# A local-attention layer with sinks: half of the queries projected first, keys and values second

## The chip, the cores and the metric

The kernel runs on one core of one Trainium2 chip. The metric is the device time of one execution of the whole program, in microseconds (us). It is a forward pass through four layers; the change touches the third of them only.

## What is computed

A sequence of 512 tokens with 1,024 features goes through four layers. Each layer is a token mixer and a convolutional feed-forward network (FFN), both between RMS norms and added to the residual h. The mixers are, in order, a sparse attention ("nsa"), a stick-breaking attention ("sb"), a local attention with sinks ("swa") and "nsa" again. The third one, cut to what matters:

```
def swa_sink_mixer(h, w_in, sinks, w_out):        # H=16 query heads, G=2 key/value heads, dh=64, W=128
    q, k, v = jnp.split(h @ w_in, [H * dh, H * dh + G * dh], axis=-1)      # 1024 | 128 | 128 columns
    ...                                           # query t sees the W keys up to t
    s = einsum(q, k window) * scale - slopes * dist
    m = jnp.maximum(max(s), sink)
    e = jnp.where(mask, jnp.exp(s - m), 0.0)
    p = e / (jnp.sum(e) + jnp.exp(sink - m))
    return (p @ v window) @ w_out
```

The layer's input is rms_norm(h) times a gain.

## The kernel before, in words

**Data.** Activations lie with features on the partitions: h, and the scaled input as eight chunks of 128 features by 512 tokens. Every f32 operand of a large product is split into a high and a low part of the reduced format (xh and xl for activations, w_hi and w_lo for weights), and a product is three matmuls: high by high, high by low, low by high. The norm's factor 1/rms of each token isn't needed for the products: it is applied afterwards, as rb (per column) or rt (per token on partitions), when a result leaves PSUM.

**Weight units.** Weights come in units of 128 x 1024 f32 through a ring of four slots (RING). SP's queue loads w_raw of a unit once the unit four before it has been split. ScalarE (ACT) makes w_hi (L252, `split_hi`), once the unit four before it has been used (units_done); VectorE (DVE) makes w_lo (L258, `split_lo`). `split_his(u, n)` and `split_los(u, n)` do this for units u+3 to u+n+2 (AHEAD is 3). On each engine everything is in program order, so a split that waits holds back what stands behind it.

**Panels.** A panel is a group of four PSUM banks, and panels alternate between the lower and the upper half of PSUM. Panel p starts when panel p-2 has been read out (`panel_free`; the table MIX_READS says which engines read each panel). The layer's query projection is two panels of four units each, 96 matmuls of 512 columns with 128 x 128 weights: 4 units x 2 chunks x 4 banks x 3. Keys and values are two units: for each of the eight chunks three matmuls of 512 columns (keys, weights stationary) and twelve of 128 columns (values, activations stationary; 4 token groups x 3).

**The start of a layer.** When the FFN before has ended, ACT forms rn (L433, L434), and then for each of the eight chunks DVE forms dh (L454) and h (L460), ACT xh (L472) and the square (L477), DVE xl (L440); GpSimd (POOL) adds up the squares (L484, L488). TensorE (PE) can follow chunk by chunk in two ways. `first_panel` uses a chunk's xh for eight matmuls (L319, L320) as soon as ACT has made it, and its xl (L323) when that is there. The other way, which the swa layer has, waits for xl of a pair of chunks (x_ready). After the last square, `pe_rsum` sums over partitions (L370) and over tokens (L373), and `act_rb` makes rt and rb (L381 to L386).

**The swa layer before.** PE: keys and values (panel p0, units u0 and u0+1), `pe_rsum`, first half of the queries (`after_rsum`, panel p0+1, L348 to L350), second half (`x_panel`, panel p0+2, L298 to L300), attention, output projection. DVE takes keys out into ktmp (L892), ACT spreads them into kh (L860), DVE makes kl (L870, L877); ACT takes out the values (L1611); DVE takes out the queries (L883). Attention waits for both query halves, k_ready and v_ready. The sb and nsa layers start with `first_panel` on queries (or keys), and so does every FFN.

Of the kernel before, what the change touches and what calls it, by code (L numbers as in the profile page):

```python
# [12 lines left out]
P = 128  # L13
# [6 lines left out]
DH = 64  # L20
# [20 lines left out]
MIX_PANELS = {"nsa": 8, "sb": 6, "swa": 3}  # L41

MIX_READS = {"nsa": [(1, 0), (1, 0), (0, 1), (1, 0), (1, 1), (0, 0), (1, 1), (0, 0)], "sb": [(1, 0)] * 4 + [(0, 1)] * 2,
             "swa": [(1, 1)] + [(1, 0)] * 2}

L1_UNITS = (8, 9, 11, 12, 14, 15, 17, 18)
QB_UNITS = (10, 13, 16, 19)
# [55 lines left out]
def hybrid_layers(nc, ins, out, kinds=KIND):  # L103
# [7 lines left out]
    with ExitStack() as ctx:  # L111
# [103 lines left out]
        def panel_free(pe, p, i=None, step=0):  # L215


            if p >= 2:
                pe.wait_ge(evac_v, at(i, step, v_after[p - 1]))
                if s_after[p - 1]:  # L220
                    pe.wait_ge(evac_s, s_after[p - 1])

        def bank(p, o):
            return psum[:, 4 * (p % 2) + o, :]
# [36 lines left out]
        def split_his(act, u, count):  # L261

            count = min(count, plan.units - AHEAD - u)
            turns = count // 4 if count >= 8 else 0
            if turns:
                with act.Fori(0, turns) as i:
                    for k in range(4):
                        split_hi(act, u + k + AHEAD, i)
            for k in range(4 * turns, count):
                split_hi(act, u + k + AHEAD)  # L270
# [95 lines left out]
        def pe_rsum(pe, n, p, by_token):  # L366

            pe.wait_ge(ssh_done, 8 * (n + 1))
            panel_free(pe, p)
            mm = nc.tensor.matmul(bank(p, 3), ones[:], ss[:], start=True, stop=True)  # L370
            if by_token:
                for t in range(TC):
                    mm = nc.tensor.matmul(bank(p, 2)[:, t:t + 1], ss[:, t * P:(t + 1) * P], ones[:, 0:1],  # L373
                                          start=(t == 0), stop=(t == TC - 1), skip_group_check=True)
            mm.then_inc(rsum_done, 1)
# [446 lines left out]
        def three(out, lh, ll, rh, rl, start, stop, **kw):  # L822

            nc.tensor.matmul(out, lh, rh, start=start, stop=False, **kw)  # L824
            nc.tensor.matmul(out, ll, rh, start=False, stop=False, **kw)  # L825
            return nc.tensor.matmul(out, lh, rl, start=False, stop=stop, **kw)  # L826
# [748 lines left out]

        def pe_swa(pe, l):
            n, u0, p0 = 2 * l, plan.mix_u[l], plan.mix_p[l]
            panel_free(pe, p0)
            for j in range(2):
                u = u0 + j  # L1580
                pe.wait_ge(split_done, u + 1)
                for q in range(4):
                    c = 4 * j + q
                    if q % 2 == 0:
                        pe.wait_ge(x_ready, 8 * n + c + 2)
                    wk, wv = slice(256 * q, 256 * q + P), slice(256 * q + P, 256 * q + 2 * P)
                    three(bank(p0, 0), w_hi[:, u % RING, wk], w_lo[:, u % RING, wk], xh[:, c, :], xl[:, c, :], c == 0, c == DC - 1)
                    for t in range(TC):
                        tok = slice(t * P, (t + 1) * P)
                        mm = three(bank(p0, 2)[:, tok], xh[:, c, tok], xl[:, c, tok], w_hi[:, u % RING, wv],  # L1590
                                   w_lo[:, u % RING, wv], c == 0 and t == 0, c == DC - 1, skip_group_check=True)
                mm.then_inc(units_done, 1)
            pe_rsum(pe, n, p0 + 1, True)
            after_rsum(pe, p0 + 1, u0 + 2, n, True)
            x_panel(pe, p0 + 2, u0 + 6, n)
            panel_free(pe, p0 + 4)
            pe.wait_ge(k_ready, kc_before[l] + 1)
            pe.wait_ge(v_ready, kvs_before[l] + 1)
            pe_attention(pe, l, "swa")
            pe_out(pe, l, ot)  # L1600

        def act_swa(act, ch, l):
            n, u0, p0 = 2 * l, plan.mix_u[l], plan.mix_p[l]
            split_his(act, u0 + 1, 1)
            act_rb(act, ch, n, p0 + 1, True)
            split_hi(act, u0 + 2 + AHEAD)
            act_k(act, l, 0, 0, 1, 2)
            for t in range(TC):
                for g in range(SG):
                    src = bank(p0, 2)[:, t * P + g * DH:t * P + (g + 1) * DH]  # L1610
                    m = ch.then(nc.scalar.activation(vt[0][:, t, g * P:(g + 1) * P].rearrange("p (e d) -> p e d", d=DH),  # L1611
                                                     src.unsqueeze(1).to_broadcast([P, 2, DH]), ACT.Copy, scale=rt[:, t:t + 1]))
            act.wait_ge(s_chain, m)
            act.sem_inc(evac_s, 1)
            act.sem_inc(v_ready, 1)
            split_his(act, u0 + 3, 7)
            act.wait_ge(k_ready, kc_before[l] + 1)
            act.wait_ge(q_done, qn_before[l] + 2)
            act.wait_ge(mix_landed, 16 * small_before[l])
            act_attention(act, l, "swa")  # L1620
            act_turn_o(act, l, plan.out_p[l])
            act_out(act, l)

        def dve_swa(dve, ch, l):
            n, u0, p0 = 2 * l, plan.mix_u[l], plan.mix_p[l]
            split_los(dve, u0 + 1, 1)
            dve.wait_ge(rb_done, n + 1)
            split_lo(dve, u0 + 2 + AHEAD)
            dve_k(dve, ch, l, 0, p0, u0 + 2, 1)
            dve.wait_ge(kt_done, kc_before[l] + 1)  # L1630
            dve.sem_inc(evac_v, 1)
            dve_k_low(dve, ch, l, 0, 0, 1, 2)
            split_los(dve, u0 + 3, 3)
            dve_q(dve, ch, l, 0, p0 + 1, u0 + 6, -SCALE, qt)
            split_los(dve, u0 + 6, 4)
            dve_q(dve, ch, l, 1, p0 + 2, u0 + 10, -SCALE, qt)
            dve.wait_ge(mix_landed, 16 * small_before[l])
            dve.wait_ge(v_chain, ch.then(nc.vector.tensor_scalar(neg_sinks[:], sinks[:], -1.0, None, ALU.mult)))
            dve_attention(dve, ch, l, "swa")
            dve_turn_o(dve, l, plan.out_p[l])  # L1640
            dve_out(dve, l)
# [315 lines left out]
def layout(x, norm_g, nsa_w_in, nsa_cmp_pos, nsa_cmp_w1, nsa_cmp_w2, nsa_w_out, sb_w_in, sb_w_out,  # L1957
           swa_w_in, swa_sinks, swa_w_out, ffn_w_up, ffn_conv_w, ffn_conv_b, ffn_w_down):

    a = {}  # L1960
    a["x"] = x[0].T.reshape(DC, P, T).transpose(1, 0, 2)
    a["norm_g"] = norm_g.reshape(DEPTH * 4, DC, P).transpose(2, 0, 1)
    a["conv_w"] = ffn_conv_w.reshape(DEPTH * 3, 2 * FC, P).transpose(2, 0, 1)
    a["conv_b"] = ffn_conv_b.reshape(DEPTH, 2 * FC, P).transpose(2, 0, 1)

    up = ffn_w_up.reshape(DEPTH, DC // 2, 2, P, 2, UP_PANELS, 256)
    a["w_up"] = up.transpose(0, 5, 1, 3, 2, 4, 6).reshape(-1, P, 1024)

    w1 = nsa_cmp_w1.reshape(-1, 2, 4, 4, P, CMP_HID).transpose(0, 1, 2, 4, 3, 5).reshape(-1, 8, P, 1024)
    a["nsa_in"] = np.zeros((len(w1) * 28, P, 1024), np.float32)  # L1970
    for j, w in enumerate(nsa_w_in):
        u = units(w[:, :2560])
        a["nsa_in"][28 * j:28 * j + 4] = u[8:12]
        a["nsa_in"][28 * j + 4:28 * j + 8] = u[:4]
        a["nsa_in"][[28 * j + x for x in L1_UNITS]] = w1[j]
        a["nsa_in"][[28 * j + x for x in QB_UNITS]] = u[4:8]
        a["nsa_in"][28 * j + 20:28 * j + 28] = u[12:]
    a["nsa_gw"] = nsa_w_in[:, :, 2560:].reshape(-1, DC, P, 48).transpose(0, 2, 1, 3)
    w2 = nsa_cmp_w2.reshape(-1, 2, 2, P, DH).transpose(1, 0, 3, 2, 4)
    a["nsa_w2k"] = np.concatenate([w2[0], w2[0]], axis=-1)  # L1980
    a["nsa_w2v"] = w2[1]
    a["nsa_pos"] = nsa_cmp_pos.reshape(-1, 2, CMP_LEN // 2, P).transpose(0, 3, 1, 2)
    a["nsa_out"] = np.concatenate([units(w) for w in nsa_w_out])
    a["sb_in"] = np.concatenate([units(w) for w in sb_w_in])
    a["sb_out"] = np.concatenate([units(w) for w in sb_w_out])
    swa_kv = swa_w_in[:, :, 1024:].reshape(-1, 2, 4, P, 256).transpose(0, 1, 3, 2, 4).reshape(-1, 2, P, 1024)
    a["swa_in"] = np.concatenate([x for kv, w in zip(swa_kv, swa_w_in) for x in (kv, units(w[:, :1024]))])
    a["swa_out"] = np.concatenate([units(w) for w in swa_w_out])
    a["sinks"] = np.broadcast_to(swa_sinks[0], (P, H))
    a["w_down"] = np.concatenate([units(w) for w in ffn_w_down])  # L1990
    return a
# [40 lines left out]
```

## Time and profile before

| | us |
|---|---|
| three runs, median (lowest, highest) | 2855.12 (2848.9, 2857.5) |
| the profiled execution, whole | 2857.26 |
| its span | 2855.5 |
| PE busy in the span | 2727.1 (96%) |
| DVE, ACT, POOL busy | 1685.5, 1205.6, 362.1 |
| PE's granted clock, mean | 0.971 of full |

The span runs from the first to the last instruction that the profile shows; 1.8 us of the execution lie around it. Start times below are us from the span's start. The swa layer's mixer begins at about 1501 and its output projection ends at about 1713. Full speed of PE's clock is 2.4 GHz, and a granted clock of 0.50 is 1.2 GHz.

### The profile page before, as it was taken

How to read it: one execution, taken by the hardware profiler on the slowest of the kernel's cores; microseconds unless marked ns; L12 is line 12 of the kernel's file. 1: busy time of each engine (PE TensorE's matmuls, PEld its weight loads, DVE VectorE, ACT ScalarE, POOL GpSimd, SP SyncE). 2: the span in 40 equal slices, each digit the busy share in tenths (PEclk: the TensorE clock that was granted, in tenths of full speed). 3: DMA queues.
4: the chain of work that ended last, by engine and by line, in shares of the span. 5: the costliest groups of instructions: out<-in, count | busy, mean ns of one | idle time of the engine just before them, and what ended most of it. 6: DMA issues, size and time to landing. Idle time of an engine off the chain costs nothing.

```text
span 2855.5 us, 38959 instructions
## 1 busy us (share of the span) xinstructions
PE 2727.1 (96%) x13616; PEld 2258.7 (79%) x13616; DVE 1685.5 (59%) x2837; ACT 1205.6 (42%) x2051; POOL 362.1 (13%) x314
## 2 busy tenths in 40 slices
PE   8989999999999999999999899999999899999997
PEld 6878878888786667888887777888878788788886
DVE  7568767764442224776525758665275787576743
ACT  4356544443223443444323644443243565444431
POOL 1012111110000000211001102111010122111100
PEclk9989999999998999999996999999999999999999
DMA  4300023333232002233322012333324000233331
GB/s 155 124 23 2 1 78 107 98 95 101 77 100 70 1 1 67 92 100 95 96 75 71 31 60 83 100 97 96 90 78 133 30 1 1 67 118 95 95 96 52
DMA packets 62200, 210.83 MB, mean 74 GB/s; under 512 B 8688, under 2 KB 10736, under 8 KB 62064
## 3 DMA queue, kind: packets, MB, share of 16 engines
q1 hardware_dynamic: 62064, 209.01, 23.7%
q8 instruction: 86, 1.41, 0.2%
q14 instruction: 50, 0.41, 0.0%
HBM read 206.88 MB, written 2.10 MB: 73 GB/s over the span
## 4 chain that ended last, share of the span: by engine, by line
PE 86%; DVE 9%; ACT 3%; issue 2%; DMA 0%; DVEq 0%; POOL 0%; SPq 0%; ACTq 0%; POOLq 0%
PE psum L298 19%; PE psum L299 19%; PE psum L300 19%; PE psum L969 5%; PE psum L959 2%; PE psum L824 2%; PE psum L1692 2%; PE psum L826 2%; PE psum L825 2%; DVE h L460 2%; PE psum L1703 2%; PE psum L1722 1%; PE psum L949 1%; DVE qs L1000 1%; PE psum L948 1%
## 5 line engine op out<-in xcount | busy, mean ns | idle before, releaser
L298 PE MATMUL psum<-xh,w_hi 128*128 128x512 f32 x1760 | 691.6, 393 | 3.0 <-DVE xl L1213 3.0
L299 PE MATMUL psum<-xh,w_lo 128*128 128x512 f32 x1760 | 686.8, 390 | 0.0
L300 PE MATMUL psum<-xl,w_hi 128*128 128x512 f32 x1760 | 686.5, 390 | 0.0
L258 DVE TENSOR_TENSOR w_lo<-w_raw,w_hi 128x1024 fp32r<-128x1024 f32 x226 | 280.5, 1253 | 532.9 <-ACT w_hi L252 530.5
L252 ACT ACTIVATE w_hi<-w_raw 128x1024 fp32r<-128x1024 f32 x226 | 235.7, 1057 | 584.8 <-PE psum L300 475.0
L298 PEld LDWEIGHTS psum<-xh,w_hi 128*128 128x128 f32 x1760 | 331.5, 188 | 74.4 <-issue 5.8
L299 PEld LDWEIGHTS psum<-xh,w_lo 128*128 128x128 f32 x1760 | 331.7, 188 | 69.9 <-issue 1.9
L300 PEld LDWEIGHTS psum<-xl,w_hi 128*128 128x128 f32 x1760 | 331.6, 188 | 69.1
L615 DVE TENSOR_TENSOR w_lo<-w_raw,w_hi 128x1024 fp32r<-128x1024 f32 x160 | 209.2, 1308 | 253.8 <-ACT w_hi L611 253.8
L298 PE MATMUL psum<-ah,w_hi 128*128 (+1 forms) x704 | 277.1, 394 | 0.0
L300 PE MATMUL psum<-al,w_hi 128*128 (+1 forms) x704 | 274.0, 389 | 0.0
L299 PE MATMUL psum<-ah,w_lo 128*128 (+1 forms) x704 | 273.9, 389 | 0.0
L611 ACT ACTIVATE w_hi<-w_raw 128x1024 fp32r<-128x1024 f32 x160 | 168.5, 1053 | 234.3 <-PE psum L300 234.3
L969 PE MATMUL psum<-v,pt 128*128 128x64 f32 x1504 | 212.4, 272 | 25.5 <-DVE pt L1072 25.3
L969 PEld LDWEIGHTS psum<-v,pt 128*128 128x128 f32 x1504 | 202.2, 194 | 42.1 <-DVE pt L1072 37.1
L585 POOL TENSOR_TENSOR cv<-cv 128x512 f32<-128x512 f32 x88 | 133.7, 1519 | 786.8 <-ACT cv L539 763.5
L1123 ACT ACTIVATE scores<-scores,mins 128x256 f32<-128x256 f32 (+1 forms) x320 | 171.4, 538 | 29.9 <-DVE mins L1017 22.6
L567 DVE SCALAR_TENSOR_TENSOR cv<-xo,conv_w,cv 128x512 f32<-128x512 f32 x176 | 169.5, 1003 | 0.6 <-DVE xo L558 0.6
L534 ACT ACTIVATE cv<-xo,conv_b,conv_w 128x512 f32<-128x512 f32 x176 | 129.2, 806 | 96.1 <-DVE xo L558 96.1
L1017 DVE CUSTOM_DVE_ANT_0 scores<-psum,tb 128x256 f32<-128x256 f32 (+1 forms) x320 | 148.8, 468 | 24.2 <-PE psum L949 22.1
L298 PEld LDWEIGHTS psum<-ah,w_hi 128*128 128x128 f32 x704 | 132.1, 188 | 29.1 <-issue 1.9
L299 PEld LDWEIGHTS psum<-ah,w_lo 128*128 128x128 f32 x704 | 132.2, 188 | 28.9 <-issue 1.9
(193 smaller groups left out, 4132.1 us busy)
## 6 DMA issues: line engine op xcount, KB each, us to landing
w_raw<-w_up SPq DMA_DIRECT2D x176, 512.0 KB, 3.6
w_raw<-w_down SPq DMA_DIRECT2D x88, 512.0 KB, 3.6
w_raw<-nsa_in SPq DMA_DIRECT2D x56, 512.0 KB, 4.0
w_raw<-sb_in SPq DMA_DIRECT2D x24, 512.0 KB, 3.7
w_raw<-nsa_out SPq DMA_DIRECT2D x16, 512.0 KB, 3.6
w_raw<-swa_in SPq DMA_DIRECT2D x10, 512.0 KB, 3.8
w_raw<-sb_out SPq DMA_DIRECT2D x8, 512.0 KB, 3.6
w_raw<-swa_out SPq DMA_DIRECT2D x8, 512.0 KB, 3.6
```

The source lines that it names most:

```text
L252: nc.scalar.activation(w_hi[:, u % RING, :], w_raw[:, u % RING, :], ACT.Copy).then_inc(hi_done, 1)
L258: nc.vector.tensor_tensor(w_lo[:, u % RING, :], w_raw[:, u % RING, :], w_hi[:, u % RING, :].bitcast(F32), ALU.subtract).then_inc(split_don ...
L298: nc.tensor.matmul(bank(p, o), wh[:, k, o, :], xhi(k), start=(first and k == 0), stop=False)
L299: nc.tensor.matmul(bank(p, o), wl[:, k, o, :], xhi(k), start=False, stop=False)
L300: mm = nc.tensor.matmul(bank(p, o), wh[:, k, o, :], xlo(k), start=False, stop=(last and k == 1))
L567: marks.append(ch.then(nc.vector.scalar_tensor_tensor(cv[:, o, :], xo[:, o, 1:T + 1], conv_w[:, 1, bass.ds(cc, 1)], cv[:, o, :], ALU.mult, ...
L585: nc.gpsimd.tensor_tensor(cv[:, 2 + a, :], cv[:, a, :], cv[:, 2 + a, :], ALU.mult).then_inc(prod_done, 1)
L611: nc.scalar.activation(w_hi[:, u % RING, :], w_raw[:, u % RING, :], ACT.Copy).then_inc(hi_done, 1)
L615: nc.vector.tensor_tensor(w_lo[:, u % RING, :], w_raw[:, u % RING, :], w_hi[:, u % RING, :].bitcast(F32), ALU.subtract).then_inc(split_don ...
L969: mm = nc.tensor.matmul(psum[:, 6 + job % 2, i * DH:(i + 1) * DH], pt[:, s % 2, j * P:(j + 1) * P], vt[b][:, k0 + j, bass.ds(it * DH, DH)] ...
L1017: x = nc.vector.tensor_tensor_reduce(out=sp_[:, s % 4, 0:nk * P], in0=psum[:, s % 4, 0:nk * P], in1=bias, scale=1.0, scalar=3e38, op0=ALU. ...
L1123: nc.scalar.activation(sp_[:, s % 4, 0:nk * P], sp_[:, s % 4, 0:nk * P], ACT.Exp, scale=-1.0, bias=mins[:, c:c + 1], accum_out=rsums[:, c: ...
```

## The change

The swa mixer's projections are put in another order. Panel p0 is the first half of the queries, with `first_panel`; then come `pe_rsum` and, as panel p0+1, keys and values (banks 0 and 1 of the panel, since banks 2 and 3 hold the sums of the norm); the second half of the queries stays last. Splits and read-outs on ACT and DVE are put in an order to match, and the weight units are laid out in the new order. The number of matmuls, splits, read-outs and DMAs is the same.

```
-             "swa": [(1, 1)] + [(1, 0)] * 2}
+             "swa": [(1, 0), (1, 1), (1, 0)]}
 def pe_swa(pe, l):
-            panel_free(pe, p0)
+            first_panel(pe, p0, u0, n)
+            pe_rsum(pe, n, p0 + 1, True)
             for j in range(2):
-                u = u0 + j
+                u = u0 + 4 + j
                 pe.wait_ge(split_done, u + 1)
                 for q in range(4):
                     c = 4 * j + q
-                    if q % 2 == 0:
-                        pe.wait_ge(x_ready, 8 * n + c + 2)
-                    three(bank(p0, 0), ...)                      # keys
+                    three(bank(p0 + 1, 0), ...)
                     for t in range(TC):
-                        mm = three(bank(p0, 2)[:, tok], ...)     # values
+                        mm = three(bank(p0 + 1, 1)[:, tok], ...)
                 mm.then_inc(units_done, 1)
-            pe_rsum(pe, n, p0 + 1, True)
-            after_rsum(pe, p0 + 1, u0 + 2, n, True)
             x_panel(pe, p0 + 2, u0 + 6, n)
 def act_swa(act, ch, l):
-            split_his(act, u0 + 1, 1)
+            split_his(act, u0 + 1, 3)
             act_rb(act, ch, n, p0 + 1, True)
-            split_hi(act, u0 + 2 + AHEAD)
+            split_his(act, u0 + 4, 3)
             act_k(act, l, 0, 0, 1, 2)
             ...                                                  # values, now from bank(p0 + 1, 1)
-            split_his(act, u0 + 3, 7)
+            split_his(act, u0 + 7, 3)
 def dve_swa(dve, ch, l):
-            split_los(dve, u0 + 1, 1)
+            split_los(dve, u0 + 1, 3)
             dve.wait_ge(rb_done, n + 1)
-            split_lo(dve, u0 + 2 + AHEAD)
-            dve_k(dve, ch, l, 0, p0, u0 + 2, 1)
+            split_lo(dve, u0 + 4 + AHEAD)
+            dve_q(dve, ch, l, 0, p0, u0 + 4, -SCALE, qt)
+            split_los(dve, u0 + 5, 2)
+            dve_k(dve, ch, l, 0, p0 + 1, u0 + 6, 1)
             ...
             dve_k_low(dve, ch, l, 0, 0, 1, 2)
-            split_los(dve, u0 + 3, 3)
-            dve_q(dve, ch, l, 0, p0 + 1, u0 + 6, -SCALE, qt)
-            split_los(dve, u0 + 6, 4)
+            split_los(dve, u0 + 7, 3)
             dve_q(dve, ch, l, 1, p0 + 2, u0 + 10, -SCALE, qt)
```

In the layout of the weights the two key/value units, which came first, stand between the four units of either query half.

## Rows read from the trace of the kernel before

**Rows 1.** The page: engines, the chain's shares, the two split groups (busy, mean ns).

```profile
PE 2727.1 (96%) x13616; PEld 2258.7 (79%) x13616; DVE 1685.5 (59%) x2837; ACT 1205.6 (42%) x2051; POOL 362.1 (13%) x314
...
PE 86%; DVE 9%; ACT 3%; issue 2%; DMA 0%; DVEq 0%; POOL 0%; SPq 0%; ACTq 0%; POOLq 0%
...
L258 DVE TENSOR_TENSOR w_lo<-w_raw,w_hi 128x1024 fp32r<-128x1024 f32 x226 | 280.5, 1253 | 532.9 <-ACT w_hi L252 530.5
L252 ACT ACTIVATE w_hi<-w_raw 128x1024 fp32r<-128x1024 f32 x226 | 235.7, 1057 | 584.8 <-PE psum L300 475.0
```

**Rows 2.** Stage windows, swa projections: length; PE, PEld, DVE, ACT, POOL busy; PE's granted clock; DMA share; GB/s.

```profile
1508.20:1539.10 30.90, 30.90 (x121) 28.58 (x122) 19.14 (x18) 8.42 (x13) 10.11 (x7) 0.50 0.06 19
1542.40:1547.80 5.40, 5.40 (x14) 4.24 (x14) 1.83 (x2) 3.27 (x6) 0.00 (x0) 0.50 0.11 6
1547.80:1588.60 40.80, 40.80 (x180) 33.49 (x179) 14.88 (x15) 13.19 (x19) 2.19 (x2) 1.00 0.32 102
```

**Rows 3.** The chain that ended last, swa projections: start, us, what.

```profile
1501.37 0.70 ACT rn L433
...
1508.20 0.76 PE psum L824
1508.96 0.43 PE psum L825
...
1512.27 0.53 PE psum L824
...
1539.15 1.81 PE psum L370 x2
...
1542.46 0.64 PE psum L348
...
1588.44 0.24 PE psum L300
...
1588.70 2.50 DVE qt L883 x4
```

**Rows 4.** The same chain where the sb layer starts, with `first_panel`.

```profile
766.84 0.70 ACT rn L433
...
770.71 0.77 PE psum L319
...
795.61 0.86 PE psum L370 x2
...
797.25 0.34 PE psum L348
```

**Rows 5.** Stage windows: longest and shortest slow start of a `first_panel`.

```profile
770.70:776.70 6.00, 5.99 (x15) 4.71 (x16) 5.23 (x9) 2.77 (x5) 0.00 (x0) 0.53 0.40 161
2087.60:2089.80 2.20, 2.18 (x5) 1.81 (x6) 2.00 (x4) 1.23 (x3) 0.00 (x0) 0.50 0.75 285
```

**Rows 6.** Timeline of PE, last nsa layer: first of 24 narrow matmuls, and the next.

```profile
2155.57 0.28 PE L824 MATMUL psum<-w_hi,xch 128*124 128x256 f32 x1
...
2158.41 0.40 PE L298 MATMUL psum<-xh,w_hi 128*128 128x512 f32 x1
```

**Rows 7.** Timeline of ACT: the last xh of the sb and of the swa layer.

```profile
791.79 0.72 ACT L472 ACTIVATE xh<-h,norm_g 128x512 fp32r<-128x512 f32 x1 [2.06 <-DVE h L460]
...
1525.84 0.72 ACT L472 ACTIVATE xh<-h,norm_g 128x512 fp32r<-128x512 f32 x1 [2.06 <-DVE h L460]
```

**Rows 8.** Stage window in the middle of the swa layer's attention.

```profile
1600.00:1656.00 56.00, 49.95 (x412) 45.44 (x411) 51.55 (x253) 48.25 (x169) 7.96 (x13) 1.00 0.01 1
```

**Rows 9.** Timelines of ACT and DVE: keys and values made ready, before.

```profile
1547.15 4.30 ACT L860 ACTIVATE kh<-ktmp 64x1024 fp32r<-64x1024 f32 x4 [1.96 <-DVE ktmp L892]
1551.48 2.18 ACT L1611 ACTIVATE v<-psum,rt 128x128 f32<-128x128 f32 x8
...
1551.49 2.47 DVE L870 TENSOR_TENSOR kl<-ktmp,kh 64x1024 fp32r<-64x1024 f32 x2 [4.37 <-ACT kh L860]
1553.99 1.39 DVE L877 CAST kl<-kl 64x1024 fp32r<-64x1024 f32 x2
```

More of the change, by code:

```diff
@@ L1583, in pe_swa @@
                     c = 4 * j + q
-                    if q % 2 == 0:
-                        pe.wait_ge(x_ready, 8 * n + c + 2)
                     wk, wv = slice(256 * q, 256 * q + P), slice(256 * q + P, 256 * q + 2 * P)
-                    three(bank(p0, 0), w_hi[:, u % RING, wk], w_lo[:, u % RING, wk], xh[:, c, :], xl[:, c, :], c == 0, c == DC - 1)
+                    three(bank(p0 + 1, 0), w_hi[:, u % RING, wk], w_lo[:, u % RING, wk], xh[:, c, :], xl[:, c, :], c == 0, c == DC - 1)
                     for t in range(TC):
                         tok = slice(t * P, (t + 1) * P)
-                        mm = three(bank(p0, 2)[:, tok], xh[:, c, tok], xl[:, c, tok], w_hi[:, u % RING, wv],
+                        mm = three(bank(p0 + 1, 1)[:, tok], xh[:, c, tok], xl[:, c, tok], w_hi[:, u % RING, wv],
                                    w_lo[:, u % RING, wv], c == 0 and t == 0, c == DC - 1, skip_group_check=True)
                 mm.then_inc(units_done, 1)
-            pe_rsum(pe, n, p0 + 1, True)
-            after_rsum(pe, p0 + 1, u0 + 2, n, True)
             x_panel(pe, p0 + 2, u0 + 6, n)
@@ L1609, in act_swa @@
                 for g in range(SG):
-                    src = bank(p0, 2)[:, t * P + g * DH:t * P + (g + 1) * DH]
+                    src = bank(p0 + 1, 1)[:, t * P + g * DH:t * P + (g + 1) * DH]
                     m = ch.then(nc.scalar.activation(vt[0][:, t, g * P:(g + 1) * P].rearrange("p (e d) -> p e d", d=DH),
@@ L1986, in layout @@
     swa_kv = swa_w_in[:, :, 1024:].reshape(-1, 2, 4, P, 256).transpose(0, 1, 3, 2, 4).reshape(-1, 2, P, 1024)
-    a["swa_in"] = np.concatenate([x for kv, w in zip(swa_kv, swa_w_in) for x in (kv, units(w[:, :1024]))])
+    a["swa_in"] = np.concatenate([x for kv, w in zip(swa_kv, swa_w_in) for x in (units(w[:, :512]), kv, units(w[:, 512:1024]))])
     a["swa_out"] = np.concatenate([units(w) for w in swa_w_out])
```

## The prediction, made before the change was run

> **What bounds the kernel now.** I read the page first. PE is busy for 96% of the span and carries 86% of the chain that ended last [rows 1], so time is won where PE waits, or where it is busy but slow. Then I cut the place of the change, the swa projections, into stage windows, and looked at the granted clock [rows 2]. The reader is to see one number there: while PE works through keys and values it is busy all 30.9 us, at a clock of 0.50, that is 1.2 GHz. It stays at 1.2 GHz through the norm's sums and 5.4 us of the first query half, and is at 2.4 GHz from 1547.8 on. So PE is slow here for 39.6 us on end, from 1508.2 to 1547.8, and every microsecond of that costs half of itself.
>
> The chain of the same stretch gives the dates [rows 3]: rn at 1501.37; first matmul at 1508.20, 6.8 us later; norm's sums at 1539.15; first query half from 1542.46 to the second's end at 1588.68; then the read-out of the queries (L883), and attention. The chain is PE without a gap from 1508.20 to 1588.68. Whatever ends the projections sooner starts attention sooner by as much, for that read-out and all behind it stay as they are.
>
> Last, I looked at how the other layers start. The sb layer's `first_panel` starts 3.87 us after its rn (770.71 less 766.84), because it needs only xh of one chunk [rows 4]. It too starts at 1.2 GHz, but is at 2.4 GHz after 6 us [rows 5]. I looked at all seven places in the trace where `first_panel` runs: the clock is back within 6 us of the first matmul in each. In the shortest the slow part is 2.2 us [rows 5].
>
> **The change, part by part.** I build the new stage from the swa layer's own rn, at 1501.37 [rows 3].
>
> 1. *Start.* Add the sb layer's 3.87 us [rows 4]: PE starts at 1505.24.
>
> 2. *First query half.* 96 matmuls of 512 columns. At full clock one takes 40.8/180 = 0.227 us [rows 2], so 21.8 us in all. A slow stretch adds half its length, 1.1 us for 2.2 us and 3.0 us for 6 us [rows 5]: PE alone would end at 1528.1 to 1530.0. The panel can also not end before its data: in the sb layer it ended 3.10 us after the last xh was there (795.61 less 791.79 + 0.72) [rows 4, 7]. The swa layer's last xh is there at 1526.56 [rows 7], which gives 1529.7. These agree; I take 1529.7. The slow start costs next to nothing here, because the wait for the chunks covers it; without that cover it costs the 3.0 us at most.
>
> 3. *Norm's sums.* The sb layer takes 1.64 us from L370 to the next panel (797.25 less 795.61) [rows 4], where the swa layer took 3.31 us at half clock (1542.46 less 1539.15) [rows 3]. PE is free at 1531.3.
>
> 4. *Keys and values at 2.4 GHz.* The trace doesn't show this. At 1.2 GHz the eight chunks have a period of 3.84 us (1539.15 less 1512.27, over seven) [rows 3]: three wide matmuls at 0.43, and twelve narrow ones at 0.213. Lower bound: everything scales, 8 x 1.92 = 15.4 us. Upper bound: nothing scales and it takes 30.7 us, which is a rival's case, below. The nearest rows are 24 matmuls of 256 columns with changing weights at full clock, 2.84 us, so 0.118 each [rows 6]. A 128-column one can't well take longer than a 256-column one, and at 1.2 GHz it takes 0.213, the time that 256 columns take there, half a wide one's 0.427; so I take the same at full clock: 8 x (3 x 0.227 + 12 x 0.118) = 16.8 us. PE is done at 1548.1. The Trainium skill ("TensorE: Matmul & The Clock Gate", section "Back-to-back issue gap") gives about 81 ns for a 128-column matmul with its weight load; by that figure an estimate would be 13.2 us and the gain 3.6 us larger. The trace's 0.118 us for a wider one, and 0.213 us at half clock, which is more than twice 81 ns, don't bear it out for these operands, and the sum doesn't use it.
>
> 5. *Second query half.* 96 x 0.227 = 21.8 us. End at 1569.9, against 1588.7 before: **18.8 us sooner**.
>
> 6. *What is hidden, and by what.* Second query half needs panel p0 read out, by a `dve_q` that stands behind rb and one split. The sums end at 1531.3; ACT's Ln and Exp follow (some 2 us), then w_hi 1.06, w_lo 1.25 [rows 1] and the read-out 2.5 [rows 3]: done at about 1538.2, with 10 us to spare before 1548.1. The unit splits keep pace: PE uses a key/value unit in 8.4 us and a query unit in 5.4, and a split takes 2.3 [rows 1]; the last, unit u0+9, is due at 1564.5 and done by 1550.6. Keys and values are now ready late: after 1548.1 come the two splits' last one (2.3), ktmp (0.7 at most), kh 4.30, kl 2.47 + 1.39 on DVE and values 2.18 on ACT [rows 9], so about 1559.5, and attention's first matmul comes after the query read-out, some 13 us later. Behind this chain wait the splits of output units, wanted only after attention. The new order hands POOL its go-ahead for the bias tables (q_done) at 1538 instead of in the second half; two short operations, of no account. DMAs are the same ten weight units, in the same ring; in the old stage they moved at 19 GB/s and less than 0.1 of the queues' time [rows 2].
>
> So the saving has these parts: 3.0 us earlier start (6.83 less 3.87), and the rest is clock. The old stage's 39.6 slow microseconds become full-speed work except for 2 to 6 us in the first panel, which gives back 17 to 19 us; of both together 2 to 3 us go to waiting for chunks.
>
> **Rivals.**
>
> *A. The clock falls again in keys and values.* For it: PE was busy through 30.9 us of just these matmuls and the clock never rose [rows 2]. Against it: holding is another thing than rising. In attention PE is at 1.00 for 56 us, with 412 matmuls that are mostly 64 to 256 columns wide, and idle for 6 us of them [rows 8]. If it fell after some 6 us: 2.9 chunks at full clock, 5.1 at 3.84 us, so the panel ends at 1557.0; the second half with 5.4 slow us at its start takes 24.5 us, end 1581.5: 7.2 us gained, 2850 for the profiled execution. Chance 7%.
>
> *B. The low clock isn't the narrow matmuls' doing, and stays* (slower). The one thing that the long slow stretch had and the other starts hadn't, beside narrow matmuls, is the longer pause ahead, 6.8 us; or there is something in this place that I don't see. The new stage holds 62.0 us of full-clock work from 1505.24 on, and a slow microsecond does half; so it ends at 1505.24 + 62.0 + half the slow time. It breaks even at 43 slow us, clock back at 1548.2, and has gained less than 0.3% if the clock comes back after 1531. Slow through keys and values: 41.0 + 3.3 + 30.7 to 1580.2, then 24.5, end 1604.7, 16 us slower: 2873. Against it: seven `first_panel` starts out of seven. Chance 4% for slower, 2% for a return in between, which leaves no change.
>
> *C. The slow stretch is a mishap of the profiled execution.* In every other stage that starts from a pause the clock came back within 6 us of busy PE, so it may do so here in most executions. As a mechanism of this kernel: the old stage would then have been held by chunks (xl of the last at 1527.4), would have ended keys and values at about 1531.7, sums at 1533.4 and both halves at 1577.0. The change would gain 7.1 us: 2848. Against it: the old runs' median is only 2.1 us under the profiled execution, where it should be 11.7 under. The lowest, 8.4 under, may be such a run in part. Chance 6%. The Trainium skill (same page, section "What's actually happening") speaks for this rival: it has the clock throttled by default and released by sustained activity. The trace disagrees, with 39.6 busy us at 1.2 GHz [rows 2].
>
> *D. A new wait*: the read-out of panel p0 or keys and values come late. Margins of 10 and 13 us have to be used up first. Chance 2%, and it would eat into the gain only.
>
> **How the numbers follow.** My forecast has 81%. By the profiled execution the time is 2857.26 - 18.8 = 2838.5; by the median of the old runs it is 2855.12 - 18.8 = 2836.3. I say 2837. Its own range takes in the spread of the old runs (6 us down, 2 up) and the 1.4 us of the lower bound in step 4: 2829 to 2841. The range of 8 in 10 is pulled up towards A and C, 2829 to 2846; above it lie most of A, B and C. Within 0.3% (8.6 us) is about what this measurement can't tell from no change. Faster 0.83 (forecast, D's larger part), same 0.12 (A, C, part of B), slower 0.05.
>
> **What would show it.** In the new profile: first matmul of the layer at rn + 3.9 us, on L319; granted clock 1.00 from about 6 us later to the end of projections; the sums at rn + 28.3; a period of 2.10 us for the key/value chunks; 21.8 us for the second half with no wait ahead of it; attention's start 18.8 us earlier against rn, everything else as it was. The forecast is wrong if the clock reads 0.50 within keys and values (A), or past 1511 (B), or if PE waits between its panels (D).

## The result, and the profile after

| | before | after |
|---|---|---|
| median of five runs each, us | 2853.82 (2845.76 to 2857.5) | 2835.03 (2832.59 to 2839.6) |
| profiled execution, us | 2857.26 | 2832.59 |
| its span, us | 2855.5 | 2830.8 |

The kernel after is faster by 18.8 us in the medians: ratio 0.9942, 95% interval 0.9922 to 0.9961. The forecast was 18.8 us and 2837. That the two figures agree to a tenth is luck: the interval allows 11 to 22 us. The two profiled executions differ by more, 24.7 us, and the first task is to say where that lies. These are rows of the page after, engines and the chain's shares, which answer to [rows 1]:

```profile
PE 2704.7 (96%) x13616; PEld 2243.4 (79%) x13616; DVE 1684.9 (60%) x2837; ACT 1204.4 (43%) x2051; POOL 361.4 (13%) x314
...
PE 85%; DVE 10%; ACT 3%; issue 2%; DMA 0%; DVEq 0%; POOL 0%; SPq 0%; ACTq 0%; POOLq 0%
```

DVE, ACT and POOL did the same work in the same time; PE lost 22.4 us of busy time with the same 13,616 matmuls. So PE's clock was higher, not its work less. Now the chain that ended last, whole span, in order of time. Each row is the last step of a norm's sum at the end of a mixer or an FFN, so differences between neighbours are the lengths of the stages. Before:

```profile
764.99 1.83 PE psum L398 x4
1128.46 1.83 PE psum L398 x4
1499.52 1.83 PE psum L398 x4
1710.83 1.83 PE psum L398 x4
2081.90 1.83 PE psum L398 x4
```

and after:

```profile
765.66 1.83 PE psum L398 x4
1120.69 1.83 PE psum L398 x4
1491.74 1.83 PE psum L398 x4
1685.52 1.83 PE psum L398 x4
2056.97 1.83 PE psum L398 x4
```

The swa mixer took 211.31 us before (1710.83 less 1499.52) and 193.78 after: 17.5 us less. The sb mixer, with not a line changed, took 363.47 and 355.03: 8.4 us less, which belongs to that execution and not to the change (last section). The FFN between them took 371.06 and 371.05. So the change's own share of the 24.7 us is 17.5.

Within the swa mixer, here are the chain's dates after, to be laid beside [rows 3]:

```profile
1493.60 0.70 ACT rn L433
...
1497.46 0.77 PE psum L319
...
1522.04 0.86 PE psum L370 x2
...
1523.68 0.34 PE psum L824
...
1525.77 0.28 PE psum L824
...
1527.81 0.28 PE psum L824
...
1540.05 0.28 PE psum L298
...
1561.94 2.49 DVE qt L883 x4
```

| step, us | forecast | measured after | how |
|---|---|---|---|
| rn to first matmul | 3.87 | 3.86 | 1497.46 - 1493.60 |
| rn to norm's sums | 28.3 | 28.4 | 1522.04 - 1493.60 |
| norm's sums | 1.64 | 1.64 | 1523.68 - 1522.04 |
| keys and values | 16.8 | 16.4 | 1540.05 - 1523.68 |
| second query half | 21.8 | 21.9 | 1561.94 - 1540.05 |
| rn to the last read-out | 68.5 | 68.3 | 1561.94 - 1493.60; before 87.3 [rows 3] |

The stage windows after (columns as in [rows 2]) show the clock that made it: 0.50 until about 1503, then 1.00 through all three panels. The last row is the start of attention, of which more below.

```profile
1497.40:1499.40 2.00, 1.94 (x5) 1.60 (x6) 1.93 (x3) 1.03 (x3) 0.00 (x0) 0.50 0.97 383
1499.40:1503.00 3.60, 3.60 (x10) 2.83 (x9) 3.28 (x5) 1.79 (x4) 0.00 (x0) 0.52 0.30 122
1503.00:1522.00 19.00, 19.00 (x85) 15.71 (x84) 16.88 (x16) 8.82 (x13) 10.23 (x7) 1.00 0.00 1
1523.60:1540.30 16.70, 16.70 (x123) 15.57 (x123) 5.51 (x7) 3.84 (x7) 1.18 (x2) 1.00 0.45 152
1540.30:1562.00 21.70, 21.60 (x96) 17.53 (x94) 9.31 (x10) 10.50 (x16) 0.00 (x0) 1.00 0.31 97
...
1566.20:1578.00 11.80, 11.13 (x53) 10.79 (x54) 7.79 (x37) 7.16 (x25) 1.23 (x2) 0.50 0.00 0
```

These are the rows over the start of attention before, where PE's first matmul is at 1593.0. Within the second the clock is at 0.50 up to 1599.0, so the slow part is 6.0 us:

```profile
1593.00:1597.80 4.80, 4.16 (x18) 3.79 (x19) 3.10 (x16) 2.60 (x9) 0.61 (x1) 0.50 0.00 0
1597.80:1600.00 2.20, 2.20 (x18) 2.20 (x17) 2.02 (x8) 1.30 (x6) 0.00 (x0) 0.73 0.00 0
```

The margins on DVE held. This is its timeline after: the first query half is read out by 1530.1, 9.9 us before PE wants its banks; kl is done at 1551.3, some 15 us before attention's first matmul at 1566.2.

```profile
1527.65 2.48 DVE L883 SCALAR_TENSOR_TENSOR qt<-psum,rb 128x512 f32<-128x512 f32 x4
...
1542.38 0.68 DVE L892 TENSOR_TENSOR ktmp<-psum,rb 128x512 f32<-128x512 f32 x1
...
1549.94 1.39 DVE L877 CAST kl<-kl 64x1024 fp32r<-64x1024 f32 x2
```

In what follows, "the stretch" is rn (L433) to the start of the queries' last read-out: 87.3 us before, 68.3 after. It is read from one profile each. The two kernels that were profiled twice have 87.3 and 86.9, and 68.3 and 68.3, where the whole time moves by over ten, so it is the measure for the experiments. "Narrow" is a 128-column matmul with new weights, "wide" one of 512 columns. In both kernels keys and values are, per chunk, twelve narrow ones and three wide.

### The profile page after: what moved, and what is told of

Same layout as the page of the kernel before. It is cut to its first block, busy times and chain, and to the rows that moved or that the text cites. A ratio compares the mean times of both kernels' runs of the same rounds, so it can differ in the third digit from the quotient of the medians.

```text
span 2830.8 us, 38964 instructions
## 1 busy us (share of the span) xinstructions
PE 2704.7 (96%) x13616; PEld 2243.4 (79%) x13616; DVE 1684.9 (60%) x2837; ACT 1204.4 (43%) x2051; POOL 361.4 (13%) x314
## 4 chain that ended last, share of the span: by engine, by line
PE 85%; DVE 10%; ACT 3%; issue 2%; DMA 0%; DVEq 0%; POOL 0%; SPq 0%; ACTq 0%; POOLq 0%
PE psum L298 19%; PE psum L300 19%; PE psum L299 19%; PE psum L969 5%; PE psum L959 2%; DVE h L460 2%; PE psum L1689 2%; PE psum L824 2%; PE psum L826 2%; PE psum L825 2%; PE psum L1700 1%; PE psum L1719 1%; PE psum L949 1%; DVE xl L440 1%; PE psum L948 1%
## 5 line engine op out<-in xcount | busy, mean ns | idle before, releaser
L298 PE MATMUL psum<-xh,w_hi 128*128 128x512 f32 x1736 | 682.7, 393 | 4.0 <-DVE xl L1213 4.0
L300 PE MATMUL psum<-xl,w_hi 128*128 128x512 f32 x1736 | 678.2, 391 | 0.0
L299 PE MATMUL psum<-xh,w_lo 128*128 128x512 f32 x1736 | 677.8, 390 | 0.0
L300 PEld LDWEIGHTS psum<-xl,w_hi 128*128 128x128 f32 x1736 | 326.9, 188 | 68.3
```

The costliest lines, as they stand in the source:

```text
L298: nc.tensor.matmul(bank(p, o), wh[:, k, o, :], xhi(k), start=(first and k == 0), stop=False)
L299: nc.tensor.matmul(bank(p, o), wl[:, k, o, :], xhi(k), start=False, stop=False)
L300: mm = nc.tensor.matmul(bank(p, o), wh[:, k, o, :], xlo(k), start=False, stop=(last and k == 1))
```

## The experiments

### Does the slow stretch come back? The kernel before, once more

No edit.

> The kernel before, unchanged, profiled a second time. Narrow-matmul theory: the slow stretch belongs to the 128-column matmuls, so keys and values again run at a granted clock of 0.50 from end to end, and from rn (L433) to the queries' last read-out (L883) it takes 87.3 us again, within 1 us. Rival C (a mishap of one execution): the clock is back within 6 us and the same stretch takes about 76 us. The sb mixer, 8.4 us longer in the profile of before than in that of after with the same code, may come out at either length.

Measured: 2850.8 us, one run. The granted clock in keys and values, and in the first query half behind them:

```profile
1499.80:1530.60 30.80, 30.80 (x121) 28.48 (x121) 19.14 (x18) 8.41 (x13) 10.11 (x7) 0.50 0.06 20
1534.00:1539.20 5.20, 5.20 (x15) 4.10 (x15) 1.83 (x2) 3.08 (x6) 0.00 (x0) 0.58 0.07 6
```

The stretch took 86.9 us. The slow keys and values are the kernel's own, and rival C (a mishap) falls. The sb mixer took 356.8 us this time, against 363.5.

### The order alone: queries first, but started by pairs

```
 def pe_swa(pe, l):                     # kernel after
-            first_panel(pe, p0, u0, n)
+            x_panel(pe, p0, u0, n)
```

> The kernel after, with the first query half waiting for pairs of chunks (as the old keys and values did) and not with first_panel: wide matmuls after the long pause of 6.8 us. Narrow-matmul theory: the clock is back within 6 us of the first matmul, and only the later start costs: rn to the queries' last read-out 71.8 us against 68.3 after, 3 to 4 us slower than after. Rival B (the longer pause keeps the clock low): 0.50 for some 39 us, the stretch takes about 88 us, no gain over before.

Measured: stretch 71.9 us; 2838.13 us in the median of four, ratio to before 0.9942 (0.9919 to 0.9965), which the whole time can't tell from after.

```profile
1496.30:1501.00 4.70, 4.51 (x11) 3.64 (x12) 4.31 (x7) 2.49 (x4) 0.53 (x1) 0.53 0.04 17
1501.00:1505.00 4.00, 4.00 (x19) 3.25 (x19) 4.00 (x3) 1.25 (x2) 3.71 (x3) 1.00 0.00 0
```

The same long pause as before is ahead of these matmuls, and the clock is back after 5 us. So the pause alone isn't what kept it low, and rival B loses one leg. The two parts of the change can now be priced: order 15.4 us (87.3 to 71.9), `first_panel` 3.6 us (71.9 to 68.3).

### The start alone: keys and values first, chunk by chunk

```
 def pe_swa(pe, l):                     # kernel before
-                    if q % 2 == 0:
-                        pe.wait_ge(x_ready, 8 * n + c + 2)
+                    pe.wait_ge(x_ready, 8 * n + c + 1)
```

> The kernel before, with keys and values waiting for one chunk at a time and not for pairs, so that PE pauses 4.6 us ahead of them and not 6.8: narrow matmuls after a short pause. Narrow-matmul theory: 0.50 until wide matmuls come again, the whole stretch 2.2 us shorter than before, about 85 us. Rival B (the long pause is the cause): clock back within 6 us, the stretch about 76 us.

Measured: stretch 84.2 us, 3.2 less than before; 2847.77 us, one run.

```profile
1497.60:1528.50 30.90, 30.88 (x121) 28.59 (x122) 21.17 (x21) 9.66 (x15) 10.11 (x7) 0.50 0.13 45
```

A shorter pause (first matmul at rn + 4.6 us) and the same 30.9 us at 0.50. Whether the pause is 4.6 or 6.8 us long makes no difference to the slow stretch behind it.

### Same place, other matmuls: values by wide matmuls, keys and values still first

```
 def pe_swa(pe, l):                     # kernel before
-                    for t in range(TC):
-                        tok = slice(t * P, (t + 1) * P)
-                        mm = three(bank(p0, 2)[:, tok], xh[:, c, tok], xl[:, c, tok], w_hi[:, u % RING, wv], ...)
+                    mm = three(bank(p0, 2), w_hi[:, u % RING, wv], w_lo[:, u % RING, wv], xh[:, c, :], xl[:, c, :], ...)
```

> The kernel before, with the twelve 128-column matmuls of each chunk replaced by three of 512 columns (weights stationary); what it leaves out: the values come out feature by token and are not turned, so attention works on wrongly laid out values. Keys and values still first, still by pairs, still after the 6.8 us pause. Narrow-matmul theory: clock back within 6 us of the first matmul, rn to last read-out 74 us. Rival B (place or pause): clock at 0.50 through the panel and into the queries, 81 us.

Measured: stretch 74.5 us; 2841.0 us, one run.

```profile
1503.30:1508.00 4.70, 4.70 (x12) 3.68 (x13) 4.31 (x7) 2.48 (x4) 0.65 (x1) 0.52 0.05 18
1508.00:1511.00 3.00, 3.00 (x14) 2.23 (x12) 3.00 (x3) 1.25 (x2) 2.71 (x3) 1.00 0.00 0
1511.10:1515.90 4.80, 0.03 (x1) 0.00 (x0) 4.60 (x5) 1.24 (x2) 2.75 (x3) 0.87 0.00 0
1516.00:1521.00 5.00, 4.95 (x12) 3.80 (x12) 4.68 (x4) 1.33 (x3) 2.42 (x2) 0.50 0.00 0
```

Same place, same pause, same pairs; only the values' matmuls are others, and the clock is back after 5 us. That closes rival B. The edit changes three things together: the values' columns (512 for 128), the number of matmuls and weight loads of a chunk (6 for 15), and the stationary operand (weights for activations). No run takes them apart. The third and fourth row bring something new: PE waits 4.8 us for the next pair of chunks, and the clock falls again.

### Do narrow matmuls hold a clock that is already up? PE busy in the pause

```
 def pe_swa(pe, l):                     # kernel before
             panel_free(pe, p0)
+            pe.wait_ge(split_done, u0 + 1)
+            for k in range(30):
+                nc.tensor.matmul(bank(p0, 1), w_hi[:, u0 % RING, 0:P], w_hi[:, u0 % RING, 0:512], start=True, stop=True)
```

> The kernel before, with 30 extra 512-column matmuls into an unused bank in the pause ahead of keys and values, so that PE comes out of the pause at full clock. Theory (narrow matmuls don't raise the clock but hold it): granted clock 1.00 through keys and values, whose pace is then set by the chunks; rn to last read-out 75.7 us, 11 to 12 us faster than before. Rival A (narrow matmuls lower the clock): it falls to 0.50 within keys and values, the stretch takes over 80 us.

Measured: stretch 83.9 us, not 75.7; 2849.45 us in the median of ten, ratio 0.9989 (0.9972 to 1.0007), no difference that can be told. By the signs set beforehand this is rival A: 0.50 within keys and values, and over 80 us. The rows show that the fall came in another way than either theory had it:

```profile
1494.80:1501.00 6.20, 6.16 (x29) 4.84 (x28) 5.76 (x9) 3.01 (x5) 0.00 (x0) 1.00 0.79 310
1501.00:1508.70 7.70, 7.55 (x56) 6.85 (x55) 7.30 (x8) 3.22 (x6) 4.33 (x3) 1.00 0.01 2
1508.80:1512.60 3.80, 0.00 (x0) 0.00 (x0) 3.60 (x5) 1.24 (x2) 1.76 (x2) 0.82 0.00 0
1512.80:1528.30 15.50, 15.50 (x61) 14.34 (x62) 6.91 (x6) 3.43 (x5) 3.72 (x3) 0.50 0.10 34
```

Keys and values began at 1500.0, and through their first 8.7 us the clock stayed at 1.00. It fell in a pause of 3.8 us in which PE waited for the third pair of chunks, and the narrow matmuls behind that pause ran 15.5 us at 0.50 without raising it. My expectation had overlooked the pause.

### The pauses between the pairs filled as well

```
 def pe_swa(pe, l):                     # the kernel above
                 for q in range(4):
                     c = 4 * j + q
+                    for k in range({4: 14, 6: 8}.get(c, 0)):
+                        nc.tensor.matmul(bank(p0, 1), w_hi[:, u % RING, 0:P], w_hi[:, u % RING, 0:512], start=True, stop=True)
```

> The kernel of the busy pause, in which the clock held for 9 us of keys and values and fell in a pause of 3.8 us between two pairs of chunks, with that pause and the next one also filled by 512-column matmuls into the unused bank (14 and 8). If the pauses lower the clock and not the narrow matmuls: 1.00 to the end of the queries, rn to last read-out 75.7 to 77 us, 10 us faster than before. If narrow matmuls lower it: it falls once more within the panel, over 80 us.

Measured: stretch 75.9 us; 2840.15 us in the median of four, ratio 0.9943 (0.9929 to 0.9957).

```profile
1494.90:1501.90 7.00, 6.95 (x35) 5.56 (x33) 6.23 (x10) 3.51 (x7) 0.00 (x0) 1.00 0.74 292
1501.90:1524.60 22.70, 21.43 (x137) 18.44 (x137) 17.98 (x16) 7.51 (x12) 10.16 (x7) 1.00 0.07 17
1524.60:1547.70 23.10, 23.10 (x106) 19.10 (x106) 9.23 (x9) 12.11 (x20) 0.00 (x0) 1.00 0.29 97
```

The old order, with 52 useless wide matmuls in its pauses, wins 11.5 us in the stretch. So most of what the old order lost was clock. Between these 75.9 us and the 71.9 us of the new order started by pairs lie 4.0 us more; the 22 matmuls that fill the pauses between pairs take 5.0 us (22 x 0.227), in which PE would otherwise wait for chunks.

### Does the hold last? Values done twice

```
 def pe_swa(pe, l):                     # kernel after
+                    for twice in range(2):
                         for t in range(TC):
                             ...        # the twelve narrow matmuls
```

> The kernel after, with every 128-column matmul of the values done twice into the same sums; what it changes: the values come out doubled. Keys and values then last 27.5 us in place of 16.5. Theory (at full clock, back to back, narrow matmuls hold it): granted clock 1.00 throughout, rn to the queries' last read-out 68.3 + 96 x 0.113 = 79.2 us. Rival A (narrow matmuls lower the clock, only later than 16.5 us): 0.50 in the second half of the panel and into the second query half, over 83 us.

Measured: stretch 79.0 us; 2845.4 us, one run.

```profile
1527.60:1554.60 27.00, 27.00 (x218) 25.91 (x218) 5.48 (x7) 3.69 (x6) 1.19 (x2) 1.00 0.27 94
1554.60:1576.50 21.90, 21.90 (x97) 17.81 (x96) 9.25 (x9) 10.66 (x16) 0.00 (x0) 1.00 0.30 96
```

27 us of mostly narrow matmuls, and no fall. Rival A is refuted up to this length. It also prices a narrow one at full clock: 10.7 us more in the stretch for 96, 0.111 us each.

### A version without narrow matmuls

```
 def pe_swa(pe, l):                     # kernel after
-                    for t in range(TC):
-                        ...                             # the twelve narrow matmuls
+                    mm = three(bank(p0 + 1, 1), w_hi[:, u % RING, wv], w_lo[:, u % RING, wv], xh[:, c, :], xl[:, c, :], ...)
             ...                                         # in the second query half, ahead of its third unit:
+                    pe.wait_ge(vu_done, 1)
+                    for t in range(TC):
+                        mm = nc.tensor.transpose(bank(p0 + 1, 2)[:, t * P:(t + 1) * P], ktmp[:, 1, t * P:(t + 1) * P], ident[:])
+                    mm.then_inc(vt_done, 1)
 def dve_swa(dve, ch, l):
+            nc.vector.tensor_tensor(ktmp[:, 1, :], bank(p0 + 1, 1), rb[:], ALU.mult).then_inc(vu_done, 1)
             ...
 def act_swa(act, ch, l):
+            act.wait_ge(vt_done, 1)
             ...
-                    src = bank(p0 + 1, 1)[...]
+                    src = bank(p0 + 1, 2)[...]          # and no factor rt
```

> A complete version made from the kernel after: the values are formed feature by token by three 512-column matmuls per chunk in place of twelve of 128 columns, DVE takes them out with the factor rb, and PE turns them with four transposes inside the second query half. Keys and values: 8 x 6 x 0.227 = 10.9 us in place of 16.5, the transposes give back about 0.6 us: rn to last read-out 63.3 us in place of 68.3, 5 us faster than after, about 2830 us.

Measured: stretch 63.3 us; 2831.91 us in the median of six (2827.36 to 2838.0), ratio to before 0.9916 (0.9904 to 0.9929). Keys and values, and the start of attention:

```profile
1528.40:1539.40 11.00, 11.00 (x50) 9.10 (x50) 5.51 (x7) 3.69 (x6) 2.26 (x2) 1.00 0.70 222
1566.00:1577.00 11.00, 10.35 (x49) 9.99 (x50) 7.02 (x34) 6.57 (x23) 1.23 (x2) 0.50 0.00 0
```

The 5.0 us came as worked out. The second row is a loss that every kernel so far has, for 6 to 12 us: PE waits 4.3 us for the queries' read-out, the clock falls, and attention's first tiles run at 0.50.

### PE busy ahead of attention, and the kernel after once more

```
 def pe_swa(pe, l):                     # the version above
             x_panel(pe, p0 + 2, u0 + 6, n, before=turn_values)
+            for k in range(17):
+                nc.tensor.matmul(bank(p0 + 1, 3), xh[:, 0, 0:P], xh[:, 0, :], start=True, stop=True)
             panel_free(pe, p0 + 4)
```

> The complete version with wide, turned values, and 17 more 512-column matmuls into an unused bank behind the second query half, in the 4.3 us pause in which PE waits for the queries' read-out. In all profiles so far attention began at 1.2 GHz and stayed there for 5 to 12 us. Theory: with the pause filled the granted clock is 1.00 from attention's first matmul; from the queries' read-out to the next rn 122 to 122.5 us in place of 124 to 125.6, about 2 to 3 us faster than the version without. Rival: PE isn't what attention's first tiles wait for, and the stretch stays within 0.5 us of 124.

> The kernel after, unchanged, beside the one above on the same chip. Projections, rn to last read-out, 68.3 us again; attention's stretch 124 to 125.5 us, by how long the clock stays low at its start; the time 2833 to 2840 us, so that the one above is 6 to 8 us faster in the median.

Measured, with attention and output projection as last read-out to next rn:

| | stretch | read-out to next rn | median (lowest, highest) | ratio to before |
|---|---|---|---|---|
| kernel after, again | 68.3 | 124.4 | 2833.48 (2830.36, 2837.22) | 0.9927 (0.9909 to 0.9945) |
| wide, turned, busy | 63.3 | 122.8 | 2827.60 (2826.07, 2829.36) | 0.9908 (0.9891 to 0.9925) |

The version with both is 5.9 us faster than after in the medians, and its slowest run is faster than after's fastest. The pause and attention's start in its profile:

```profile
1556.40:1560.70 4.30, 3.85 (x17) 2.84 (x16) 3.43 (x7) 1.26 (x2) 0.00 (x0) 1.00 0.04 15
1560.70:1572.00 11.30, 8.71 (x71) 7.98 (x72) 9.74 (x47) 8.74 (x30) 1.67 (x3) 1.00 0.01 2
```

Attention's first 11 us are at 1.00, and no other of the twelve profiles has less than 124.0 us from read-out to next rn. The gain from that, 1.6 to 2.8 us against 124.4 and 125.6, is small beside 11 slow microseconds. The rows fit with PE waiting there for other engines once it is fast: at full clock it is busy for 8.71 of 11.30 us, at half clock for 10.35 of 11.00. The expectation of 122 to 122.5 us was a little too low, and 5.9 us is just short of the 6 to 8 expected of the medians.

## Why the prediction was right, point by point

- *Where the time lies.* Right. I read 39.6 us of PE busy at 1.2 GHz as the kernel's loss. The kernel before has nearly all of them again in its second profile, and filling the pauses of the old order wins 11.5 us, though it adds 52 matmuls.
- *Start (step 1), sums (step 3), second half (step 5).* Each within 0.1 us, since each had a row of the same code elsewhere.
- *First query half (step 2).* The two bounds, PE's own 1528.1 to 1530.0 and the data's 1529.7, were both near: norm's sums came at rn + 28.44, forecast 28.3. The slow start (5.5 us at 0.50) was covered by the wait for chunks as said: the repeat of after, in whose profile the clock was back sooner, has the same stretch of 68.3 us. One reading was off: the shortest slow start [rows 5] is 2.9 us and not 2.2, since the clock is at 0.50 until 2090.5 and the window stops at 2089.8; and the program's first `first_panel`, at 10.3, starts at 1.00. That moves the lower of PE's two bounds by 0.4 us and not the 1529.7, which came from the data.
- *Keys and values at full clock (step 4).* 16.4 us against 16.8. The forecast took 0.118 us for a narrow matmul, from a row of 256 columns. The period of 2.04 us (1527.81 less 1525.77) gives (2.04 - 3 x 0.227)/12 = 0.113. Between the lower bound of 15.4 and the 16.8 taken it lies nearer the latter. The Trainium skill's 81 ns ("TensorE: Matmul & The Clock Gate", section "Back-to-back issue gap") would have made it 13.2 us; these runs have 0.111 to 0.113 us per narrow matmul, and disagree with it.
- *The sum.* 18.8 forecast; 19.0 in the stretch, 17.5 in the whole mixer. The 1.5 us between these were lost at the start of attention, which the forecast took to stay as it was: after the same pause of 4.3 us it ran 11.8 us at 0.50 in this profile and 6.0 us (1593.0 to 1599.0) in that of before. The twelve profiles bear this out. From read-out to next rn they take 122.8 us with no slow time there (17 matmuls in the pause), 124.0 to 124.4 with 6.0 to 6.8 slow us (five profiles), 124.8 with 8.9, 125.0 with 10.2, and 125.4 to 125.6 with 11.7 or 11.8 (four). The new order needn't be the cause: after's second profile has 6.8 slow us, and the old order with the busy pause 11.8. So the projections give 19.0 us and a profile can lose up to about 1.5 of them again behind; the 18.8 of the medians is the sum of both and of the sb layer's spread. In the second set of runs the medians are 20.8 us apart (2854.28 less 2833.48).
- *Split of the gain.* I had called 3.0 us the earlier start and the rest clock, less 2 to 3 us of waiting. The runs give 15.4 for the order and 3.6 for `first_panel`. Same mechanism, cut at another place.
- *Rivals.* A falls by after's own row of keys and values at 1.00 and by the values done twice, B by wide matmuls in the old place, C by the repeat, D by the margins of 9.9 and 15 us in after's profile. The rule of the Trainium skill that was named at C ("TensorE: Matmul & The Clock Gate", section "What's actually happening"), that activity releases the throttle, isn't borne out for this stream: in three executions with narrow matmuls first, PE was busy for 31 us each and stayed at 0.50.
- *Chances.* The recorded ones don't add up: forecast and rivals come to 102% (81, 7, 4, 2, 6, 2), and A, C and the part of B that leaves no change make 15%, where "same" has 12%.
- *What stays open.* Why keys and values, once behind a pause, don't raise the clock is not settled, nor which of their traits counts: the 128 columns, the number of weight loads, or activations as the stationary operand. A third of their time was wide matmuls (1.3 of 3.84 us per chunk). In attention's first tiles, with matmuls of 64 to 256 columns, the clock did come back, in 6 to 12 us.

## What to carry to other kernels

Read the granted clock of each stage beside PE's busy share: a PE that is 100% busy at 0.50 is a loss that no busy share, wait or chain shows. Where PE comes out of a pause, put wide matmuls first and narrow ones behind them; in this kernel that order was worth 15 us with no work removed. Pauses of 3.8 to 4.8 us lowered the clock again here, so a pause in front of narrow matmuls cost more than its length, and useless wide matmuls into a free bank are a cheap way to test whether clock is what is lost.

## What the runs showed of the hardware that I had not expected

- Once the clock was down, keys and values (per chunk twelve matmuls of 128 columns, each with new weights, and three of 512) left it at 1.2 GHz: 30.9 us on end, in three profiles, and 15.5 us behind a pause in a fourth. Once it was up, the same matmuls kept it at 2.4 GHz for 27 us.
- The length of the sb mixer, the same code in all twelve profiles, went from 355.0 to 363.5 us. Here are the windows over its heads, before and after:

```profile
909.00:1079.00 170.00, 168.06 (x816) 111.89 (x816) 42.77 (x81) 80.19 (x66) 7.02 (x12) 0.89 0.00 1
```

```profile
909.00:1071.00 162.00, 159.43 (x814) 107.72 (x815) 42.15 (x81) 79.80 (x67) 7.02 (x12) 0.94 0.00 1
```

  The clock dips at other places in one execution than in the other (960 to 980: 0.91 before, 1.00 after; 980 to 1000: 1.00 and 0.94), 0.89 and 0.94 in the mean, and PE's busy time is 8.6 us longer in the first. These 8.5 us are a large part of the 12 to 14 us by which runs of one kernel differ: before's two profiled executions are 6.5 us apart in the whole and 6.7 in the sb mixer, after's 3.6 and 5.0. So a change of 3 us, such as the busy pause alone, can't be told by whole times here but is plain in the stage.
